# The order of splits, values and transposes at four layer boundaries of a two-block network on one core

## The chip, the cores and the metric

The kernel runs on one core of a Trainium2 chip. A core has five engines that run beside each other and meet only at semaphores: PE (TensorE, matrix products and transposes, writing to the accumulator memory `ps` of 8 banks), ACT (ScalarE), DVE (VectorE), POOL (GpSimd) and SP (SyncE, which here only issues the loads of the weights). Each engine takes its instructions in the order in which they are written for it. An instruction that waits for a semaphore keeps everything behind it on its engine waiting.

The metric is the device time of one execution in microseconds (us). Before the change three runs gave 1217.36, 1217.41 and 1218.13 us, median 1217.41 us.

## The reference

For 256 tokens of width 1024 the network computes two blocks in float32, one after the other, in seven stages: a gated feed-forward layer (FFN1), a mixing layer, a second gated layer (FFN2), then an attention layer (MoBA), a squared-ReLU layer (MLP1), a differential attention layer and a second squared-ReLU layer (MLP2). The four feed-forward layers are the ones that matter here:

```python
def _swiglu(x, w_in, w_out):            # FFN1, FFN2; hidden width 2816
    g, u = jnp.split(x @ w_in, 2, axis=-1)
    return (jax.nn.silu(g) * u) @ w_out

def sq_relu_mlp(h, w_up, w_down):       # MLP1, MLP2; hidden width 4096
    return jnp.square(jax.nn.relu(h @ w_up)) @ w_down

h = _swiglu(_rms_norm(x, ffn1_pre_norm[l]), ffn1_w_in[l], ffn1_w_out[l])
x = x + 0.5 * _rms_norm(h, ffn1_post_norm[l])
...
y = sq_relu_mlp(h, mlp_w_up[i], mlp_w_down[i])
x = layer_norm(DEEPNORM_ALPHA * x + (1.0 + gate2) * y, ln_g[i, 1], ln_b[i, 1])
```

## The kernel before

**Splitting.** Every float32 operand of a product is split into a high part, which the PE format holds, and the low rest. A product is three products: high by high, low by high, high by low (`three`, L506 to L508). Weights come in units of 128 x 2048 values (1 MB), N_UNITS in all, in a ring of six slots. Per unit SP issues the load (`w_raw`), ACT makes the high part (`split_hi`, L1047, `hi_w`), DVE the low part (`split_lo`, L1520, `lo_w`), and PE multiplies. SP may load a unit when PE has finished the one six before it. PE waits for a unit's low part (`low_ready`). A unit is 24 products: the 256 tokens are two tiles of 128, and each tile takes 12.

**The gated layer** (`swiglu`, one function of that name on each engine) goes over 11 blocks of 256 hidden columns. For a block PE multiplies two units (gate and up); ACT takes the silu of the gate (`activation`, L1152); DVE multiplies it with the up part (`product`, L1788, the tile `hid`); PE transposes the result (`hidden_T`, L634) into `ps`; ACT takes the high part of the transposed block (`hidden_hi`, L1160) and DVE the low part (`hidden_lo`, L1744); then PE multiplies it with the block's unit of the second weight. The last three blocks' second products are kept for the end (`down_tail`): first block N_FF - 3 on tile 0, then the transposes of block N_FF - 1, then blocks N_FF - 2 and N_FF - 1 on tile 0, then all three on tile 1. In what follows "the last block" is N_FF - 1 and "the last unit" is the weight unit that belongs to it (`next_unit - 1`).

At the end of the layer the written orders of ACT and DVE are:

```python
# ACT                                     # DVE
split_hi(next_unit - 1)                   split_lo(next_unit - 1)
hidden_hi(b0 + N_FF - 2, ...)             hidden_lo(b0 + N_FF - 2, ...)
activation(b0 + N_FF - 1, ...)            product(b0 + N_FF - 1, ...)
hidden_hi(b0 + N_FF - 1, ...)             if sums is not None: sums()
split_hi(next_unit)                       hidden_lo(b0 + N_FF - 1, ...)
split_hi(next_unit + 1)                   split_lo(next_unit), split_lo(next_unit + 1)
```

`sums` is `first_modulation`, in FFN2 alone: 15 small DVE instructions (L1777 to L1918) that finish the modulation vectors of the second block of the network. After these rows follows `after_rms`: DVE scales the layer's output out of `ps` (`rms_part`, L1603), computes the norm of tile 0, adds it to `x` (L1615), splits one more unit and then the new stage's input (`quarter_split`, L1553 to L1559). PE transposes `x` (`x_quarter_T`, L585) as two groups of four between the last products of `down_tail`, and waits for the L1615 half that each group reads.

**The squared-ReLU layer** (`mlp`) begins with `entry`: units 0, 1 and 2 of the layer for tile 0, then for tile 1. Units 0 and 1 give block 0 (banks 4 and 5), units 2 and 3 block 1 (banks 6 and 7). After `entry` PE transposes block 0 (`hidden_T(b0, 0, 4)`, eight transposes, L634), which waits for DVE's square (`product`, L1839); then it multiplies unit 3 for both tiles (`in_unit(u0 + 3, ...)`) and then units 4 and 5 with block 0's transposed values, for which it waits for `hidden_lo`. In MLP1 DVE also has pieces of a modulation product to do between its splits (L1757, L1760, L1767), right behind `hidden_lo`.

The code that matters:

Of the kernel before, what the change touches and what calls it, by code (L numbers as in the profile page):

```python
# [23 lines left out]
N_FF = D_FF // FF_B  # L24
# [119 lines left out]
def turned_up(j):  # L144
    return 4 * N_NAT - 2 + 2 * j - (j == N_TURN - 1)
# [6 lines left out]
def ring_slot(u):  # L152
    return u % RING
# [20 lines left out]
def two_blocks_kernel(nc, d, out):  # L174
    with ExitStack() as ctx:
# [108 lines left out]
        ffn_hT = [(hT_hi, hT_lo, 0), (hT_hi, hT_lo, 2), (hT2_hi, hT2_lo, 0)]  # L284
# [215 lines left out]
        def _(pe):  # L500
# [114 lines left out]
            def entry(u0, b, src):  # L615

                def second_tile_T():
                    x_quarter_T(b, 1, 0, src)
                    x_quarter_T(b, 1, 1, src)

                first_three = [(u0, 0, 0), (u0 + 1, 0, 1), (u0 + 2, 1, 0)]
                for u, block, half in first_three:
                    entry_unit(u, b, 0, block, half, second_tile_T if src is zt and block == 1 else None)
                    if src is x and half == 1:
                        second_tile_T()
                for u, block, half in first_three:
                    entry_unit(u, b, 1, block, half)
# [14 lines left out]
            def hidden_T(b, i, chunks):  # L642

                pe.wait_ge(hid_done, b + 1)
                transposes(hid, 0, chunks, (4 + 2 * (i % 2)) * BANK).then_inc(hidT, 1)
# [19 lines left out]
            xT = (xT_hi, xT_lo)  # L665
# [32 lines left out]
            def mlp(s, u0, b0, t0):  # L698
                def up_turned(j):

                    u, pair = u0 + turned_up(j), 4 + 2 * (j % 2)
                    if j < 2:
                        pe.wait_ge(hidT_lo, b0 + j + 1)
                    else:
                        pe.wait_ge(up_sum, t0 + j - 1)
                    low_ready(u)
                    whi = hi_w[:, ring_slot(u), :].rearrange("p (k f) -> p k f", k=KD)
                    wlo = lo_w[:, ring_slot(u), :].rearrange("p (k f) -> p k f", k=KD)
                    for f in range(2):
                        dst, cols = bank(pair + f), slice(f * P, (f + 1) * P)  # L710
                        for k in range(KD):
                            both = xT_both[:, k, :, :].rearrange("p s n -> p (s n)")
                            if k > 0:
                                pe.matmul(dst[:, 0:SEQ], wlo[:, k, cols], xT_hi[:, k, :], start=False, stop=False)  # L714
                            mm = pe.matmul(dst, whi[:, k, cols], both, start=k == 0, stop=k == KD - 1)  # L715
                            if k == 0:
                                pe.matmul(dst[:, 0:SEQ], wlo[:, k, cols], xT_hi[:, k, :], start=False, stop=False)
                    mm.then_inc(w_used, 1)

                def down_turned(j):  # L720
                    pe.wait_ge(turned_lo_done, t0 + j + 1)
                    down_unit(u0 + turned_down(j), turned_hT[j % 4], 0, False)

                entry(u0, s, zt)
                hidden_T(b0, 0, 4)
                in_unit(u0 + 3, xT, 4, [6, 7], False, True)
                for half in range(2):
                    pe.wait_ge(hidT_lo, b0 + 1)
                    down_unit(u0 + 4 + half, mlp_hT[0], 2 * half, half == 0)
                hidden_T(b0 + 1, 1, 4)  # L730
                for j in range(2):
                    up_turned(j)
                    pe.wait_ge(hidT_lo, b0 + 2)
                    down_unit(u0 + 7 + 2 * j, mlp_hT[1], 2 * j, False)
                for j in range(2, N_TURN - 2):
                    up_turned(j)
                    down_turned(j - 2)
                up_turned(N_TURN - 2)
                up_turned(N_TURN - 1)
                down_turned(N_TURN - 4)  # L740
                down_tail(s, [(u0 + turned_down(j), turned_hT[j % 4], 0, t0 + j) for j in range(N_TURN - 3, N_TURN)],
                          lambda: None, None if s == S_MLP2 else zt, turned_lo_done)
# [298 lines left out]
        def _(act):  # L1041
# [103 lines left out]
            def swiglu(u0, b0, n, between=None):  # L1145
# [33 lines left out]
                    if i == 3 and between is not None:  # L1179
                        between()  # L1180
                next_unit = u0 + 3 * N_FF
                split_hi(next_unit - 1)
                hidden_hi(b0 + N_FF - 2, N_FF - 2)
                activation(b0 + N_FF - 1, N_FF - 1)
                hidden_hi(b0 + N_FF - 1, N_FF - 1)
                split_hi(next_unit)
                split_hi(next_unit + 1)
# [319 lines left out]
        def _(vec):  # L1507
# [272 lines left out]
            def swiglu(u0, b0, first, p0, n_pieces, between=None, sums=None):  # L1780
# [34 lines left out]
                    if i == 3 and between is not None:  # L1815
                        between()
                next_unit = u0 + 3 * N_FF
                split_lo(next_unit - 1)
                hidden_lo(b0 + N_FF - 2, N_FF - 2, 2, ffn_hT[(N_FF - 2) % 3])
                product(b0 + N_FF - 1, N_FF - 1)  # L1820
                if sums is not None:
                    sums()
                hidden_lo(b0 + N_FF - 1, N_FF - 1, 2, ffn_hT[(N_FF - 1) % 3])
                split_lo(next_unit)
                split_lo(next_unit + 1)

# [675 lines left out]
```

## Time and profile before

| | |
|---|---|
| device time, median of 3 runs | 1217.41 us |
| the profiled execution: from its first to its last instruction (the only time that its page gives) | 1216.0 us |
| PE busy | 1199.6 us (99%), 5805 products and transposes |
| DVE busy | 950.8 us (78%) |
| ACT busy | 620.2 us (51%) |
| mean granted clock of PE | 0.997 of full |
| the chain that ended last | PE 88%, DVE 4%, ACT 3%, DMA 2% |
| data moved | 274.31 MB, mean 226 GB/s |

In the rows below a time is in us from the first instruction. A row of a timeline gives the start, the duration, the engine, the line, the operation, what it writes and reads, its shape, how many instructions it joins, and in brackets how long the engine had been idle before it and what ended that. Ends of PE instructions are modelled: products that follow each other show 0.39 us each and start 0.23 us apart. So a row's idle time on PE is counted from a modelled end. On ACT and DVE an instruction usually starts about 0.1 us before the end shown for the one ahead of it.

### The profile page before, as it was taken

How to read it: one execution, taken by the hardware profiler on the slowest of the kernel's cores; microseconds unless marked ns; L12 is line 12 of the kernel's file. 1: busy time of each engine (PE TensorE's matmuls, PEld its weight loads, DVE VectorE, ACT ScalarE, POOL GpSimd, SP SyncE). 2: the span in 40 equal slices, each digit the busy share in tenths (PEclk: the TensorE clock that was granted, in tenths of full speed). 3: DMA queues.
4: the chain of work that ended last, by engine and by line, in shares of the span. 5: the costliest groups of instructions: out<-in, count | busy, mean ns of one | idle time of the engine just before them, and what ended most of it. 6: DMA issues, size and time to landing. Idle time of an engine off the chain costs nothing.

```text
span 1216.0 us, 14811 instructions
## 1 busy us (share of the span) xinstructions
PE 1199.6 (99%) x5805; PEld 984.3 (81%) x5805; DVE 950.8 (78%) x1373; ACT 620.2 (51%) x844; POOL 83.0 (7%) x130
## 2 busy tenths in 40 slices
PE   9999999999999999999999999999999999999997
PEld 7888888888778888888887777888888777888885
DVE  7789878876766689889786668898998888765656
ACT  7345336445774464334465656443446565643441
POOL 2110130000300010000000000000100000000000
PEclk9999999999999999999999999999999999999998
DMA  9999995644645489989466347788856634566540
GB/s 317 352 319 321 311 300 185 221 143 155 200 157 175 156 295 349 317 307 333 150 219 225 106 127 254 269 305 281 312 193 215 217 114 139 174 217 216 185 162 35
DMA packets 145205, 274.31 MB, mean 226 GB/s; under 512 B 6240, under 2 KB 76080, under 8 KB 145136
## 3 DMA queue, kind: packets, MB, share of 16 engines
q1 hardware_dynamic: 127280, 209.80, 51.3%
q0 software_dynamic: 17792, 63.56, 15.2%
q8 instruction: 46, 0.75, 0.2%
q14 instruction: 23, 0.19, 0.0%
q10 hardware_dynamic: 64, 0.02, 0.0%
HBM read 270.41 MB, written 2.93 MB: 225 GB/s over the span
## 4 chain that ended last, share of the span: by engine, by line
PE 88%; DVE 4%; ACT 3%; DMA 2%; issue 2%; POOL 0%; ACTq 0%; DVEq 0%; POOLq 0%
PE ps L506 23%; PE ps L508 23%; PE ps L507 23%; PE ps L715 7%; PE ps L714 3%; PE ps L634 2%; DMA w_raw<-in_ffn_w_out 1%; ACT hi_w L1047 1%; DVE lo_w L1520 1%; PE ps L585 1%; PE ps L931 1%; DMA area<-rel_scratch 1%; ACT aux L1078 1%; PE ps L910 1%; PE ps L792 1%
## 5 line engine op out<-in xcount | busy, mean ns | idle before, releaser
L1520 DVE TENSOR_TENSOR lo_w<-w_raw,hi_w 128x2048 fp32r<-128x2048 f32 x195 | 443.5, 2287 | 65.7 <-ACT hi_w L1047 65.1
L1047 ACT ACTIVATE hi_w<-w_raw 128x2048 fp32r<-128x2048 f32 x195 | 370.3, 1916 | 46.6 <-DMA w_raw<-in_ffn_w_in 12.3
L506 PE MATMUL ps<-hi_w,xT 128*128 128x512 f32 x912 | 364.3, 399 | 2.2 <-DVE xT L1554 2.2
L508 PE MATMUL ps<-lo_w,xT 128*128 128x512 f32 x912 | 356.0, 390 | 0.0
L507 PE MATMUL ps<-hi_w,xT 128*128 128x512 f32 x912 | 355.3, 390 | 0.0
L506 PEld LDWEIGHTS ps<-hi_w,xT 128*128 128x128 f32 x912 | 171.3, 188 | 41.5 <-issue 8.1
L508 PEld LDWEIGHTS ps<-lo_w,xT 128*128 128x128 f32 x912 | 171.1, 188 | 37.0
L507 PEld LDWEIGHTS ps<-hi_w,xT 128*128 128x128 f32 x912 | 171.5, 188 | 33.4
L506 PE MATMUL ps<-hi_w,hT_hi 128*128 128x512 f32 x480 | 188.3, 392 | 0.0
L508 PE MATMUL ps<-lo_w,hT_hi 128*128 128x512 f32 x480 | 186.9, 389 | 0.0
L507 PE MATMUL ps<-hi_w,hT_lo 128*128 128x512 f32 x480 | 186.8, 389 | 0.0
L715 PE MATMUL ps<-xT,hi_w 128*128 128x512 f32 x384 | 134.6, 396 | 0.0
L508 PEld LDWEIGHTS ps<-lo_w,hT_hi 128*128 128x128 f32 x480 | 90.1, 188 | 19.1
L507 PEld LDWEIGHTS ps<-hi_w,hT_lo 128*128 128x128 f32 x480 | 90.1, 188 | 18.5
L506 PEld LDWEIGHTS ps<-hi_w,hT_hi 128*128 128x128 f32 x480 | 90.1, 188 | 18.0 <-issue 0.7
L714 PE MATMUL ps<-xT,lo_w 128*128 128x256 f32 x336 | 93.7, 279 | 0.0
L1760 DVE SCALAR_TENSOR_TENSOR piece_acc<-aux,c_act,piece_acc 128x512 f32<-128x512 f32 x119 | 89.3, 751 | 3.7
L1212 ACT ACTIVATE area<-ps 128x512 f32<-128x512 f32 x24 | 14.3, 597 | 135.3 <-PE ps L715 135.3
L715 PEld LDWEIGHTS ps<-xT,hi_w 128*128 128x128 f32 x384 | 70.2, 188 | 13.8
L1160 ACT ACTIVATE hT_hi<-ps 128x512 fp32r<-128x512 f32 x22 | 13.1, 598 | 107.2 <-PE ps L634 107.2
L714 PEld LDWEIGHTS ps<-xT,lo_w 128*128 128x128 f32 x336 | 63.3, 189 | 2.1
L1845 DVE TENSOR_TENSOR area<-ps,area 128x512 f32<-128x512 f32 x24 | 16.5, 689 | 48.8 <-ACT area L1212 48.8
(275 smaller groups left out, 1041.6 us busy)
## 6 DMA issues: line engine op xcount, KB each, us to landing
w_raw<-in_ffn_w_in SPq DMA_DIRECT2D x86, 512.0 KB
aux<-in_ada_w POOLq DMA_DIRECT2D x34, 1024.0 KB, 7.9
w_raw<-in_mlp_w_up SPq DMA_DIRECT2D x32, 1024.0 KB
w_raw<-in_mlp_w_down SPq DMA_DIRECT2D x32, 1024.0 KB
w_raw<-in_w_mix_in SPq DMA_DIRECT2D x26, 1024.0 KB
w_raw<-in_ffn_w_out SPq DMA_DIRECT2D x22, 1024.0 KB
area<-in_ada_w POOLq DMA_DIRECT2D x14, 1024.0 KB, 5.8
w_raw<-in_moba_w_in SPq DMA_DIRECT2D x12, 1024.0 KB
```

The costliest lines, as they stand in the source:

```text
L506: pe.matmul(dst, lhs_hi, rhs_hi, start=start, stop=False)
L507: pe.matmul(dst, lhs_lo, rhs_hi, start=False, stop=False)
L508: return pe.matmul(dst, lhs_hi, rhs_lo, start=False, stop=stop)
L634: mm = pe.transpose(ps[:, off:off + P], src[:, t, col0 + c * P:col0 + (c + 1) * P], ident[:, :])
L714: pe.matmul(dst[:, 0:SEQ], wlo[:, k, cols], xT_hi[:, k, :], start=False, stop=False)
L715: mm = pe.matmul(dst, whi[:, k, cols], both, start=k == 0, stop=k == KD - 1)
L1047: act.activation(hi_w[:, ring_slot(u), :], w_raw[:, ring_slot(u), :], ACT.Copy).then_inc(w_hi, 1)
L1160: act.activation(hi[:, c0:c0 + 2, :], ps[:, off:off + 2 * SEQ].rearrange("p (c n) -> p c n", c=2), ACT.Copy).then_inc(hidT_hi, 1)
L1212: act.activation(turned_lo, pair[:, :, 1, :], ACT.Copy).then_inc(up_low, 1)
L1520: vec.tensor_tensor(lo_w[:, ring_slot(u), :], w_raw[:, ring_slot(u), :], hi_w[:, ring_slot(u), :].bitcast(F32), ALU.subtract).then_inc(w_l ...
L1760: ins = vec.scalar_tensor_tensor(out=acc, in0=row, scalar=c_act[:, c:c + 1], in1=acc, op0=ALU.mult, op1=ALU.add)
L1845: vec.tensor_tensor(turned_sum, pair[:, :, 0, :], turned_lo, ALU.add).then_inc(up_sum, 1)
```

## The change

Three places are edited. In `mlp` on PE the two tiles of unit 3 (the layer's fourth) are taken apart and the transposes of block 0 stand between them. In the gated layer's end on ACT and on DVE, `split_hi` and `split_lo` of the last unit are written behind `activation` and `product` of the last block, and on DVE the last block's `hidden_lo` is written ahead of `sums`.

```diff
@@ PE, mlp
                 entry(u0, s, zt)
+                in_unit(u0 + 3, xT, 4, [6, 7], False, True, tiles=[0])
                 hidden_T(b0, 0, 4)
-                in_unit(u0 + 3, xT, 4, [6, 7], False, True)
+                in_unit(u0 + 3, xT, 4, [6, 7], False, True, tiles=[1])
@@ ACT, swiglu
                 next_unit = u0 + 3 * N_FF
-                split_hi(next_unit - 1)
                 hidden_hi(b0 + N_FF - 2, N_FF - 2)
                 activation(b0 + N_FF - 1, N_FF - 1)
+                split_hi(next_unit - 1)
                 hidden_hi(b0 + N_FF - 1, N_FF - 1)
@@ DVE, swiglu
                 next_unit = u0 + 3 * N_FF
-                split_lo(next_unit - 1)
                 hidden_lo(b0 + N_FF - 2, N_FF - 2, 2, ffn_hT[(N_FF - 2) % 3])
                 product(b0 + N_FF - 1, N_FF - 1)
+                split_lo(next_unit - 1)
+                hidden_lo(b0 + N_FF - 1, N_FF - 1, 2, ffn_hT[(N_FF - 1) % 3])
                 if sums is not None:
                     sums()
-                hidden_lo(b0 + N_FF - 1, N_FF - 1, 2, ffn_hT[(N_FF - 1) % 3])
                 split_lo(next_unit)
```

No instruction is added or taken away on any engine, and SP's order of loads is as it was. Line numbers behind the first edit are one higher in the changed kernel.

ACT at the end of FFN2 (FFN1's end reads the same): `hT_hi` is the high part of a transposed block, `area<-ps,rstd_x` the silu, `hi_w` a unit's high part. Before:

```order
L1047 ACTIVATE hi_w<-w_raw 128x2048 x2
L1160 ACTIVATE hT_hi<-ps 128x512
L1152 ACTIVATE area<-ps,rstd_x 128x256 x2
L1160 ACTIVATE hT_hi<-ps 128x512
L1047 ACTIVATE hi_w<-w_raw 128x2048 x2
```

And now:

```order
L1048 ACTIVATE hi_w<-w_raw 128x2048
L1161 ACTIVATE hT_hi<-ps 128x512
L1153 ACTIVATE area<-ps,rstd_x 128x256 x2
L1048 ACTIVATE hi_w<-w_raw 128x2048
L1161 ACTIVATE hT_hi<-ps 128x512
L1048 ACTIVATE hi_w<-w_raw 128x2048 x2
```

One of the two splits ahead has moved behind the last silu.

DVE at the end of FFN2: `lo_w` is a unit's low part, `hT_lo` that of a transposed block, `area<-ps,rstd_x,area` the product of silu and up part, `mod_cols` and `aff_*` the modulation. Before:

```order
L1520 TENSOR_TENSOR lo_w<-w_raw,hi_w 128x2048 x2
L1744 TENSOR_TENSOR hT_lo<-ps,hT_hi 128x512
L1788 SCALAR_TENSOR_TENSOR area<-ps,rstd_x,area 128x256 x2
L1777 TENSOR_TENSOR mod_cols<-ps,adab_cols 32x64 x4
...
L1918 TENSOR_TENSOR aff_b<-aff_b,mod_cols 128x8
L1744 TENSOR_TENSOR hT_lo<-ps,hT_hi 128x512
L1520 TENSOR_TENSOR lo_w<-w_raw,hi_w 128x2048 x2
L1603 SCALAR_TENSOR_TENSOR area<-ps,area 128x512 x2
```

And now:

```order
L1521 TENSOR_TENSOR lo_w<-w_raw,hi_w 128x2048
L1745 TENSOR_TENSOR hT_lo<-ps,hT_hi 128x512
L1789 SCALAR_TENSOR_TENSOR area<-ps,rstd_x,area 128x256 x2
L1521 TENSOR_TENSOR lo_w<-w_raw,hi_w 128x2048
L1745 TENSOR_TENSOR hT_lo<-ps,hT_hi 128x512
L1778 TENSOR_TENSOR mod_cols<-ps,adab_cols 32x64 x4
...
L1919 TENSOR_TENSOR aff_b<-aff_b,mod_cols 128x8
L1521 TENSOR_TENSOR lo_w<-w_raw,hi_w 128x2048 x2
L1604 SCALAR_TENSOR_TENSOR area<-ps,area 128x512 x2
```

One split now stands behind the product, and the modulation instructions stand between the last block's low part and the splits for the next stage.

On PE, in each of the two squared-ReLU layers, the eight transposes of block 0 now stand 12 products later than before, and nothing else differs.

## Rows read from the trace of the kernel before

**Rows 1.** What PE waited for, whole span: engine line, releaser, us in total, times, longest

```profile
PE ps L506 <- DVE xT L1554: 2.2, 2, 1.1
...
PE ps L634 <- DVE area L1788: 0.4, 1, 0.4
PE ps L634 <- DVE area L1839: 0.4, 2, 0.3
```

**Rows 2.** Timeline of PE at the end of FFN1

```profile
172.92 0.39 PE L508 MATMUL ps<-lo_w,xT 128*128 128x512 f32 x1
...
173.15 0.60 PE L634 MATMUL ps<-ident,area 128*128 128x128 f32 x4
...
182.39 0.66 PE L634 MATMUL ps<-ident,area 128*128 128x128 f32 x4 [0.43 <-DVE area L1788]
```

**Rows 3.** Timeline of ACT at the end of FFN1

```profile
176.71 1.92 ACT L1047 ACTIVATE hi_w<-w_raw 128x2048 fp32r<-128x2048 f32 x1 [6.16 <-DMA w_raw<-in_ffn_w_out]
...
179.28 0.84 ACT L1152 ACTIVATE area<-ps,rstd_x 128x256 f32<-128x256 f32 x2 [0.18 <-PE ps L508]
183.08 0.60 ACT L1160 ACTIVATE hT_hi<-ps 128x512 fp32r<-128x512 f32 x1 [2.96 <-PE ps L634]
```

**Rows 4.** Timeline of DVE at the end of FFN1

```profile
178.66 2.29 DVE L1520 TENSOR_TENSOR lo_w<-w_raw,hi_w 128x2048 fp32r<-128x2048 f32 x1 [5.78 <-ACT hi_w L1047]
...
181.47 0.87 DVE L1788 SCALAR_TENSOR_TENSOR area<-ps,rstd_x,area 128x256 f32<-128x256 f32 x2
...
185.52 4.49 DVE L1520 TENSOR_TENSOR lo_w<-w_raw,hi_w 128x2048 fp32r<-128x2048 f32 x2 [1.11 <-ACT hi_w L1047]
```

**Rows 5.** Timeline of ACT at the end of FFN2

```profile
586.20 3.71 ACT L1047 ACTIVATE hi_w<-w_raw 128x2048 fp32r<-128x2048 f32 x2
...
596.83 0.84 ACT L1152 ACTIVATE area<-ps,rstd_x 128x256 f32<-128x256 f32 x2 [4.88 <-PE ps L508]
```

**Rows 6.** Timeline of DVE at the end of FFN2

```profile
597.70 0.88 DVE L1788 SCALAR_TENSOR_TENSOR area<-ps,rstd_x,area 128x256 f32<-128x256 f32 x2 [4.45 <-ACT area L1152]
598.49 0.91 DVE L1777 TENSOR_TENSOR mod_cols<-ps,adab_cols 32x64 f32<-32x64 f32 x4
...
601.17 0.69 DVE L1744 TENSOR_TENSOR hT_lo<-ps,hT_hi 128x512 fp32r<-128x512 f32 x1
602.90 4.49 DVE L1520 TENSOR_TENSOR lo_w<-w_raw,hi_w 128x2048 fp32r<-128x2048 f32 x2 [1.04 <-ACT hi_w L1047]
607.31 1.28 DVE L1603 SCALAR_TENSOR_TENSOR area<-ps,area 128x512 f32<-128x512 f32 x2
...
610.41 1.42 DVE L1615 SCALAR_TENSOR_TENSOR x<-area,rstd,x 128x512 f32<-128x512 f32 x2
```

**Rows 7.** Timeline of PE where it first transposes the output of FFN2

```profile
610.97 0.39 PE L508 MATMUL ps<-lo_w,hT_hi 128*128 128x512 f32 x1
611.22 0.66 PE L585 MATMUL ps<-ident,x 128*128 128x128 f32 x4
```

**Rows 8.** Timeline of PE at the start of MLP1 (first three) and MLP2

```profile
749.18 1.09 PE L634 MATMUL ps<-ident,area 128*128 128x128 f32 x8 [0.26 <-DVE area L1839]
...
755.60 0.39 PE L506 MATMUL ps<-hi_w,hT_hi 128*128 128x512 f32 x1
...
772.96 0.39 PE L506 MATMUL ps<-hi_w,hT_hi 128*128 128x512 f32 x1
...
1045.84 1.09 PE L634 MATMUL ps<-ident,area 128*128 128x128 f32 x8 [0.15 <-DVE area L1839]
```

**Rows 9.** Timeline of DVE at the start of MLP1

```profile
751.37 1.23 DVE L1744 TENSOR_TENSOR hT_lo<-ps,hT_hi 128x1024 fp32r<-128x1024 f32 x1
...
769.02 1.22 DVE L1744 TENSOR_TENSOR hT_lo<-ps,hT_hi 128x1024 fp32r<-128x1024 f32 x1
```

**Rows 10.** Windows at the end: stretch, length, busy of PE, PEld, DVE, ACT, POOL, PEclk, DMA, GB/s

```profile
1207.50:1209.50 2.00, 0.00 (x0) 0.00 (x0) 1.93 (x3) 0.00 (x0) 0.00 (x0) 1.00 0.35 131
1210.00:1210.50 0.50, 0.00 (x0) 0.00 (x0) 0.50 (x2) 0.22 (x1) 0.00 (x0) 0.50 0.00 0
```

## The prediction

> **What bounds the kernel now.** I read the list of PE's waits first. PE is busy nearly all the time, so an edit of order can only win what PE still waits for, and three of those waits stand where the change works: one of 0.4 us behind L1788 and two of together 0.4 us behind L1839 [rows 1]. The other large entry, 2.2 us in two waits for `xT` (L1554), belongs to the starts of MLP1 and MLP2, ahead of the edited lines, and stays. That gives a ceiling for the gain before anything else is known.
>
> An idle time on PE is counted from a modelled end. Where nothing is waited for, transposes start 0.23 us after the last product's start (172.92 to 173.15 [rows 2]), though the product is drawn 0.39 us long. So a wait costs 0.39 - 0.23 = 0.16 us more than the row says: 0.43 + 0.16 = 0.59 us at the end of FFN1 [rows 2], 0.26 + 0.16 = 0.42 us at the start of MLP1 and 0.15 + 0.16 = 0.31 us at the start of MLP2 [rows 8]. FFN2's end has no such wait. The ceiling is 0.59 + 0.42 + 0.31 = 1.32 us.
>
> Then I read ACT, DVE and PE side by side at each of the four places, since on ACT and DVE an instruction holds up all that is written behind it.
>
> **End of FFN1, term 1.** The last unit's load lands late: ACT waits 6.16 us for it and starts the split at 176.71 [rows 3]. DVE follows at 178.66 with 2.29 us and only then makes the last block's product, at 181.47 for 0.87 us, which PE awaits at 182.39 [rows 2, 4]. Now the silu comes first. It is bound by PE, at 179.28 [rows 3], so it stays there; the product follows 0.87 us later, as in FFN2 (596.83 to 597.70 [rows 5, 6]): 180.15 + 0.87 = 181.0. PE is due at 182.39 - 0.59 = 181.80. The wait goes whole.
>
> What is late next: the last unit. Silu till 180.0, split 1.92 till 181.9, low part till 184.2, the last block's low part (0.69 [rows 6]) till 184.9. PE needs both after four transposes (0.4) and 12 products (12 x 0.23): 181.8 + 0.4 + 2.8 = 185.0. It fits by 0.1 to 0.2 us. The chain that follows (ACT's next high part at 183.08 [rows 3], DVE's next splits at 185.52 [rows 4]) starts from PE's transposes, so it moves up by the same 0.59 if the mixing layer's first two units have landed by then. They had at 183.6 and 185.4; whether they had 0.6 us sooner no row shows. Bounds: -0.59 and 0; I take -0.59, because the two splits ran back to back at 185.52 without a wait for a load.
>
> **End of FFN2, term 2.** Here the load is early. ACT does both splits from 586.20, ten microseconds ahead of the silu at 596.83 [rows 5], in time in which neither ACT nor DVE has anything else: DVE stands idle 4.45 us before its product [rows 6]. The change takes one split out of this free time and puts it behind the product, where DVE has little. Step by step, each instruction starting about 0.1 us before the drawn end of the one ahead:
> - ACT: silu till 597.6, split till 599.5.
> - DVE: product at 597.70 as before. Then it waits for the high part: low part of the unit from 599.50 (a split's low part starts some 1.95 after its high part) for 2.2 us to 601.7; low part of the last block, 0.61 on, to 602.3 (before it started at 601.17). PE needs these after its next 12 products, at about 603.0: in time.
> - The modulation instructions took from 598.49 to 601.17, 2.68 us [rows 6]. Before, they lay in the time in which PE and ACT made the last block's transposes and high part. Now: 602.32 + 2.68 = 605.00.
> - The next two splits start at 605.00 where they started at 602.90, after an idle 1.04 us which is used up [rows 6]. That is +2.10.
> - From there to L1615 DVE has no gap (602.90, 607.31, 610.41 [rows 6]): L1603 at 609.41, the first half of `x` from 612.51 to 613.2.
>
> Who waits for that: PE. The first L585 group starts at 611.22, 0.25 after the product before it [rows 7], so it is due at 611.20; its input was ready at 610.41 + 0.7 = 611.11, less than 0.1 us ahead. There is no cover at all. Now PE starts at about 613.26: +2.06 us. The rest of that stage hangs on the same DVE chain, moved by 2.10, and on PE, moved by 2.06, so it adds 0.04 at most. Nothing later gives it back: no later wait of PE in [rows 1] is for something that runs by its own clock; loads are released by PE's own progress. Bounds: 0, if DVE found the modulation's time elsewhere, and 2.10. I take +2.06.
>
> One row shows how strictly such a queue holds: in FFN1 ACT idled 6.16 us till 176.71 for a load, with the transposes of 173.15 already done for the instruction behind it [rows 2, 3]. The Trainium skill (Perfetto Trace Analysis, section Tensor Engine Instruction) says that ScalarE and VectorE are strict first-in first-out and that only the tensor engine may pull weight loads ahead. It is a rule against this change, and by it the sum keeps its +2.06; if ready instructions could pass a waiting one, that term would be near nothing.
>
> **Start of MLP1 and MLP2, terms 3 and 4.** The transposes come 12 products later, 12 x 0.227 = 2.72 us. PE then never waits for the square: it starts tile 0 of unit 3 at 749.18 - 0.42 = 748.76 and is at the transposes at 751.48, when the square has been ready since 749.13. The whole 0.42 goes, and 0.31 in MLP2. Unit 3 itself was split before the square.
>
> What is late next is `hidden_lo`, which PE needs at 755.60 - 0.42 = 755.18 [rows 8]. It started 751.37 - 749.18 = 2.19 us after the transposes [rows 8, 9]: 751.48 + 2.19 = 753.67, plus 1.23 is 754.9. It fits by 0.25 us, and likewise in MLP2. But in MLP1 DVE's queue behind it is full up to block 1's `hidden_lo`, 769.02 - 751.37 = 17.65 us later [rows 9]: now 753.67 + 17.65 + 1.23 = 772.55 plus 0.05 for the semaphore, and PE needs it at 772.96 - 0.42 = 772.54 [rows 8]. That gives back 0.06. Term 3 is -0.36 (bounds -0.42 and +0.1 if a load for the modulation comes later too), term 4 -0.31 (bounds -0.31 and 0).
>
> **The sum.** -0.59 + 2.06 - 0.36 - 0.31 = +0.80 us. On the profiled execution's span of 1216.0 us that is 1216.8. The median of the runs is 1217.41, 1.4 us more than the span, for what lies outside of the first and the last instruction; this part is untouched. So 1217.41 + 0.80 = 1218.2 us, slower by 0.07%. A measurement of this kernel can tell about 0.2%, or 2.4 us, from no change; this is not to be told.
>
> **The rivals.**
> - *The change does what its parts promise and no more.* If DVE's end of FFN2 has slack that I misread (the x chain's 0.1 us, the split's idle time), only the waits go: -1.3, 1216.1 us. For it: PE shows no wait at that place before. Against it: DVE's rows leave no gap from 602.90 to the transposes. Chance 0.12.
> - *The loss stays and the gains do not.* In FFN1 the mixing units' loads land no sooner, or the 0.1 us fits of FFN1, MLP1 and MLP2 fail and PE waits for low parts in place of products. Then +2.06 with gains of 0 to 0.5: 1217.41 + 1.8 = 1219.2 us. For it: every fit is tight, and FFN1's last load came 6 us late [rows 3]. Against it: the splits at 185.52 ran without a wait. Chance 0.12.
> - *The clock falls, and the change costs over 0.2%.* The place is the new gap at the end of FFN2. PE would stand 1.9 us (613.26 less the modelled end, 611.36), then do only four transposes. In the trace the clock was still full over 2.0 us of an empty PE after the last product, and at 0.50, which is 1.2 of 2.4 GHz, when PE had been empty for 2.5 to 3 us [rows 10]. My gap is just inside the first stretch; the case decides if the real one comes out longer than that. No row has a product at the low level; twice the spacing over 12 products would be 12 x 0.23 = 2.8 us more: 1218.2 + 2.8 = 1221.0. Chance 0.05. The Trainium skill (TensorE: Matmul & The Clock Gate, section HAM oscillation — how this bites in real kernels) says that a gap in PE's work can drop it to the half clock and that the kernel then pays each time for warming up; by the same page (Part 4: PE-mode transpose) transposes do not count as such work. By that rule the transposes would lengthen the gap.
>
> **How the numbers follow.** The forecast, with FFN2's loss and most gains, has 0.68; its own range is 1217.5 to 1218.8. The rivals have 0.12, 0.12 and 0.05, and 0.03 is left for what I do not see. The range 1216.2 to 1219.8 holds the forecast, the second rival and about half of the first. Faster by over 2.4 us would need more than all waits at the edited places: 0.01. Slower by over 2.4 us is the clock's case and part of the second and of the rest: 0.08. Within: 0.91.
>
> **What would show it.** In the profile after: PE's waits behind L1789 and L1840 are gone; a new wait of about 1.9 us stands before L585, for DVE's L1616, at about 612 us; DVE's L1604 in FFN2 follows the modulation instructions with two splits and no idle time; DVE's block-1 `hT_lo` in MLP1 starts about 2 us later than now. The prediction is wrong in its main step if L585 shows no wait there, and in its small ones if PE waits for `hT_lo` or `lo_w` at the other three places. A granted clock under 1.00 near 613 us would speak for the last rival.

## The result, and the profile after

The changed kernel takes 1219.65 us (median of 21 executions, 1218.34 to 1221.22), the kernel before in the same series 1217.59 us (21 executions, 1216.79 to 1219.07). The ratio is 1.0017 with a 95% interval of 1.0011 to 1.0022: slower by 2.06 us. The forecast was 0.80 slower, 1218.2. The direction was right, but the loss is two and a half times as large. The measured time lies inside the stated range by 0.15 us only, and outside of the forecast's own 1217.5 to 1218.8. The forecast also held the change too small to be told from none; with 21 executions of each kernel the interval lies above 1.

The profiled execution of the changed kernel spans 1217.8 us, that of before 1216.0. The first two rows of after's list of PE's waits (engine line, releaser, us in total, times, longest):

```profile
PE ps L506 <- DVE xT L1555: 2.2, 2, 1.1
PE ps L585 <- DVE x L1616: 2.0, 1, 2.0
```

Both rows before L634 that the change aims at, three waits [rows 1], are off the list, and a new wait of 2.0 us stands before L585. The rest is found by reading the same places as before.

**End of FFN1.** ACT, DVE and PE of after:

```profile
178.93 0.84 ACT L1153 ACTIVATE area<-ps,rstd_x 128x256 f32<-128x256 f32 x2 [4.89 <-PE ps L508]
179.65 1.92 ACT L1048 ACTIVATE hi_w<-w_raw 128x2048 fp32r<-128x2048 f32 x1
```
```profile
179.80 0.88 DVE L1789 SCALAR_TENSOR_TENSOR area<-ps,rstd_x,area 128x256 f32<-128x256 f32 x2 [5.04 <-ACT area L1153]
...
184.52 4.49 DVE L1521 TENSOR_TENSOR lo_w<-w_raw,hi_w 128x2048 fp32r<-128x2048 f32 x2
```
```profile
181.45 0.60 PE L634 MATMUL ps<-ident,area 128*128 128x128 f32 x4
```

The product follows the silu by 0.87 us and no longer the load's split; PE starts its transposes without idle time. The next two splits start 1.00 us sooner than in [rows 4]; 0.35 of that is this execution's earlier start (its transposes before these came at 172.80, in before at 173.15), the other 0.65 is the wait of 0.59 that is gone and 0.06 that has no name here.

**End of FFN2.** DVE of after, to be laid beside [rows 6]:

```profile
596.73 0.88 DVE L1789 SCALAR_TENSOR_TENSOR area<-ps,rstd_x,area 128x256 f32<-128x256 f32 x2 [5.03 <-ACT area L1153]
598.54 2.29 DVE L1521 TENSOR_TENSOR lo_w<-w_raw,hi_w 128x2048 fp32r<-128x2048 f32 x1 [0.93 <-ACT hi_w L1048]
600.75 0.68 DVE L1745 TENSOR_TENSOR hT_lo<-ps,hT_hi 128x512 fp32r<-128x512 f32 x1
601.35 0.91 DVE L1778 TENSOR_TENSOR mod_cols<-ps,adab_cols 32x64 f32<-32x64 f32 x4
...
603.92 4.48 DVE L1521 TENSOR_TENSOR lo_w<-w_raw,hi_w 128x2048 fp32r<-128x2048 f32 x2
608.43 1.29 DVE L1604 SCALAR_TENSOR_TENSOR area<-ps,area 128x512 f32<-128x512 f32 x2
...
611.54 1.42 DVE L1616 SCALAR_TENSOR_TENSOR x<-area,rstd,x 128x512 f32<-128x512 f32 x2
```

Everything here starts 0.97 us earlier on the clock of the span, by its earlier start and the wait won in FFN1 (597.70 to 596.73). Counted from the product, the next two splits come 7.19 us later (603.92 less 596.73) and came 5.20 later before (602.90 less 597.70): +1.99. On the way to L1616 0.11 more is added (7.62 us against 7.51). From 598.54 on DVE has no idle time over 0.04 us. The forecast had +2.10 for the first part and nothing for the second: the modulation took 2.57 us here (601.35 to 603.92) in place of the 2.68 that it counted.

PE of after at the new wait, to be laid beside [rows 7]:

```profile
610.00 0.39 PE L508 MATMUL ps<-lo_w,hT_hi 128*128 128x512 f32 x1
612.35 0.65 PE L585 MATMUL ps<-ident,x 128*128 128x128 f32 x4 [1.96 <-DVE x L1616]
612.76 0.63 PE L506 MATMUL ps<-hi_w,hT_hi 128*128 128x512 f32 x1
613.19 0.63 PE L507 MATMUL ps<-hi_w,hT_lo 128*128 128x512 f32 x1
...
615.32 1.06 PE L585 MATMUL ps<-ident,x 128*128 128x128 f32 x4
616.03 0.61 PE L506 MATMUL ps<-hi_w,hT_hi 128*128 128x512 f32 x1
616.48 0.39 PE L507 MATMUL ps<-hi_w,hT_lo 128*128 128x512 f32 x1
...
623.10 1.03 PE L585 MATMUL ps<-ident,x 128*128 128x128 f32 x8
```

The last row is the next group of eight transposes. In the kernel before it is this one:

```profile
620.38 1.18 PE L585 MATMUL ps<-ident,x 128*128 128x128 f32 x8
```

Two things are to be seen. The wait is where the forecast put it. And behind it the products stand 0.43 us apart in place of 0.23, until 616.48; the second four transposes are drawn 1.06 us long, where before's at 613.10 are drawn 0.60. The windows of PE there (stretch, length, PE busy, granted clock, DMA share, GB/s) say why:

```profile
606.00:612.00 6.00, 4.39 (x20) 1.00 0.13 14
612.00:612.50 0.50, 0.15 (x1) 1.00 0.56 127
612.50:613.00 0.50, 0.50 (x5) 0.92 0.89 319
613.00:616.00 3.00, 3.00 (x11) 0.50 0.65 251
616.00:616.50 0.50, 0.50 (x4) 0.66 0.00 0
616.50:622.00 5.50, 5.50 (x26) 1.00 0.99 338
```

The granted clock was 1.00 through the idle time, fell to 0.50 (1.2 of 2.4 GHz) just as the products had begun again, and was back at 1.00 from 616.5. A window's mean tells the moment: 0.92 over half a microsecond is a fall at 612.9, which is 2.9 us after the start of the last product ahead of the gap, and 0.66 is a return at 616.3. That is the mechanism of the third rival, on top of the forecast and not in its place.

**Start of MLP1.** PE and DVE of after beside [rows 8, 9]:

```profile
754.04 1.03 PE L634 MATMUL ps<-ident,area 128*128 128x128 f32 x8
...
757.65 0.39 PE L506 MATMUL ps<-hi_w,hT_hi 128*128 128x512 f32 x1
...
775.03 0.50 PE L506 MATMUL ps<-hi_w,hT_hi 128*128 128x512 f32 x1
```
```profile
756.17 1.23 DVE L1745 TENSOR_TENSOR hT_lo<-ps,hT_hi 128x1024 fp32r<-128x1024 f32 x1 [2.22 <-ACT hT_hi L1204]
...
773.76 1.22 DVE L1745 TENSOR_TENSOR hT_lo<-ps,hT_hi 128x1024 fp32r<-128x1024 f32 x1
```

No idle time before the transposes; `hT_lo` is done at 757.40, a quarter of a microsecond ahead of L506 at 757.65; for block 1 it is done at 774.98, and PE, which started its product before that at 774.75 and was due at 774.98, starts at 775.03: the 0.05 late that the forecast counted as 0.06.

**The ledger.** Lengths on PE between the same instructions in both profiled executions, in us:

| from, to | before | after | difference | forecast |
|---|---|---|---|---|
| FFN1, transposes of the last block but one to those of the last | 9.24 | 8.65 | -0.59 | -0.59 |
| FFN2, transposes of the last block to the first L585 | 11.39 | 13.49 | +2.10 | +2.06 |
| that L585 to the next group of eight | 9.16 | 10.75 | +1.59 | 0 |
| MLP1, first L585 to the transposes of block 1 (`hidden_T(b0 + 1, 1, 4)`) | 37.76 | 37.25 | -0.51 | -0.42 |
| MLP2, the same | 37.99 | 37.62 | -0.37 | -0.31 |
| all the rest, first product to last | | | -0.06 | 0 |

MLP1's stretch ends ahead of the product that is 0.05 late; taken up to that product (772.96 in before, 775.03 here) the difference is -0.49, and the forecast's -0.36.

From the first product of FFN1 (10.90 in before) to the last it is 1196.18 before and 1198.34 after: +2.16. (The spans differ by 1.8, since the first product of this execution came 0.39 us sooner.)

### The profile page after: what moved, and what is told of

Its sections match the earlier page's. It is cut to its first block, busy times and chain, and to the rows that moved or that the text cites. A ratio compares the mean times of both kernels' runs of the same rounds, so it can differ in the third digit from the quotient of the medians.

```text
span 1217.8 us, 14811 instructions
## 1 busy us (share of the span) xinstructions
PE 1200.8 (99%) x5805; PEld 986.0 (81%) x5805; DVE 950.5 (78%) x1373; ACT 620.4 (51%) x844; POOL 83.1 (7%) x130
## 4 chain that ended last, share of the span: by engine, by line
PE 90%; DVE 5%; ACT 2%; issue 2%; DMA 0%; ACTq 0%; DVEq 0%
PE ps L506 24%; PE ps L508 24%; PE ps L507 24%; PE ps L715 7%; PE ps L714 3%; PE ps L634 2%; ACT hi_w L1048 1%; DVE lo_w L1521 1%; PE ps L585 1%; PE ps L932 1%; PE ps L911 1%; PE ps L793 1%; PE ps L909 1%; ACT area L1331 1%; DVE area L2017 0%
## 5 line engine op out<-in xcount | busy, mean ns | idle before, releaser
L506 PE MATMUL ps<-hi_w,xT 128*128 128x512 f32 x912 | 364.1, 399 | 2.2 <-DVE xT L1555 2.2
L506 PEld LDWEIGHTS ps<-hi_w,xT 128*128 128x128 f32 x912 | 171.3, 188 | 41.6 <-issue 7.9
L506 PE MATMUL ps<-hi_w,hT_hi 128*128 128x512 f32 x480 | 189.0, 394 | 0.0
L506 PEld LDWEIGHTS ps<-hi_w,hT_hi 128*128 128x128 f32 x480 | 90.4, 188 | 18.7 <-issue 0.9
```

Source lines behind the costliest of these rows:

```text
L506: pe.matmul(dst, lhs_hi, rhs_hi, start=start, stop=False)
```

## The experiments

All times are medians with the lowest and highest execution and, in brackets, the number of executions. The three series (e1 to e4, e5 to e8, e9 to e11) ran on three chips, so each ratio is to the kernel before on the same chip. The kernel before, run beside them three times, gave 1217.53 (e1 to e4), 1217.51 (e5 to e8) and 1217.45 us (e9 to e11).

### e1: the changed kernel again

> The changed kernel once more, on the chip of the next three. Theory (queue and clock): DVE's modulation work now stands ahead of the next stage's splits at the end of FFN2, PE stands 2.0 us before L585, the granted clock falls to 0.50 about 2.5 us after the last product, and seven products and four transposes run at half speed: span about 1.8 us over before, and the runs scatter, because the low clock lasts longer or shorter. Rival (queue alone): 0.8 us over before, with no scatter.

1219.79 us, 1218.43 to 1221.30 (11), ratio 1.0019 (1.0010 to 1.0027). Its trace has the wait of 1.95 us before L585 and the next group of eight 10.74 us later (10.75 in after). The loss repeats.

### e2: two unread products in the gap

```diff
 # PE, down_tail
                 if src is x and i < 2:
+                    if i == 0 and s == S_FFN2:
+                        for _ in range(2):
+                            pe.matmul(ps[:, 5 * BANK:5 * BANK + SEQ], piece_acc[:, 0, 0:P],
+                                      piece_acc[:, 0, SEQ:2 * SEQ], start=True, stop=True)
                     x_quarter_T(s + 1, 0, i, src)
```

> The changed kernel with two float32 products of 128 x 256 whose result nobody reads, on PE ahead of the first transposes of x at the end of FFN2, inside the wait. They need about 1.5 us of the 2.1. Queue and clock: the wait for DVE's x stays (L585 starts as late as in the changed kernel), the clock stays at 1.00, and the time is 1.6 us under the changed kernel, 0.5 to 0.8 us over before. Queue alone, where the low clock is only a companion of something else that slows PE: no gain, or a loss of the products' time.

1218.54 us, 1218.22 to 1220.35 (11), ratio 1.0010 (1.0001 to 1.0018): 1.25 below e1. PE of this kernel (each unread product is recorded as two instructions):

```profile
610.67 1.02 PE L573 MATMUL ps<-piece_acc 128*128 128x256 f32 x4
612.79 0.66 PE L589 MATMUL ps<-ident,x 128*128 128x128 f32 x4 [1.09 <-DVE x L1620]
613.20 0.48 PE L506 MATMUL ps<-hi_w,hT_hi 128*128 128x512 f32 x1
613.51 0.39 PE L507 MATMUL ps<-hi_w,hT_lo 128*128 128x512 f32 x1
```

The queue's part stays (13.49 us from the last block's transposes to this group, as in after), and the clock's part goes: products at 0.23 us and 9.16 us to the next group, as before. So the loss has two parts, and the second can be taken away alone. Four of the eleven executions still lie at 1219.5 to 1220.4.

### e3 and e4: FFN2 left as before

e3 is the changed kernel with the written order of before in FFN2 alone (`if u0 == U_FFN1` around the moved lines); e4 has the edit of the squared-ReLU layers alone.

> The change with the end of FFN2 left as before: the new order at the end of FFN1 and the new place of the transposes in MLP1 and MLP2. Queue and clock: -0.59 (FFN1), -0.42 (MLP1; -0.36 if the block-1 low part comes late as in the changed kernel) and -0.31 (MLP2): 1.3 us under before, no wait of PE before L585. Rival (the gains are absorbed by loads that come no sooner): the same time as before within 0.3 us.

> Only PE's edit in MLP1 and MLP2. Both theories: -0.42 or -0.36 and -0.31, together 0.7 us under before; in MLP1 DVE's block-1 low part is ready 0.05 us after PE wants it. If the transposes' later place costs more than it frees (the low part late for units 4 and 5): a wait of PE for hT_lo at the first product of unit 4.

e3: 1216.37 us, 1216.11 to 1217.45 (11), ratio 0.9990 (0.9981 to 0.9999). e4: 1216.42, 1216.05 to 1217.83 (11), ratio 0.9991 (0.9982 to 1.0000). The loss sits in FFN2 and the rest of the change gains. In e3's trace FFN1's stretch is 8.65 us, FFN2's 11.39, MLP1's 37.30 and MLP2's 37.59. But e4 was to be 0.6 slower than e3 and is not. In its trace FFN1's stretch is 8.91 us, though e4 has the old order there: the wait that the forecast read as 0.59 was 0.26 here. Nor was e4 to gain more than 0.7, and it gained 1.1; its trace has 0.89 of that at MLP1 and MLP2 (37.28 and 37.58 us). The rest no trace shows.

### e5: only the low part ahead of the modulation

```diff
 # DVE, swiglu, from before
                 product(b0 + N_FF - 1, N_FF - 1)
+                hidden_lo(b0 + N_FF - 1, ...)
                 if sums is not None:
                     sums()
-                hidden_lo(b0 + N_FF - 1, ...)
```

> The kernel before with one edit in FFN2 alone: DVE's low part of the last block stands ahead of the modulation instructions, the last unit's split stays early. If an instruction that waits holds up all behind it: DVE idles from 598.5 till the high part is there (600.97 in before), low part till 601.6, the modulation's 2.66 us till 604.3, the next splits start at 604.3 to 604.4 in place of 602.90, and PE's L585 is 1.4 to 1.5 us late. The clock then decides the rest. If a gap has to be about as long as in the changed kernel (L585 2.1 us late) to lower it, products behind L585 keep 0.23 us spacing and the median is before +1.5, about 1219.0. If any gap of this kind with only transposes behind it lowers the clock, some 1.6 us more: 1220.6. Rival to the queue (DVE finds the modulation's time elsewhere): no change, 1217.5.

1218.80 us, 1218.14 to 1220.18 (11), ratio 1.0010 (1.0001 to 1.0019): 1.3 over before. DVE of this kernel:

```profile
597.67 0.88 DVE L1788 SCALAR_TENSOR_TENSOR area<-ps,rstd_x,area 128x256 f32<-128x256 f32 x2 [4.46 <-ACT area L1152]
601.08 0.69 DVE L1744 TENSOR_TENSOR hT_lo<-ps,hT_hi 128x512 fp32r<-128x512 f32 x1 [2.52 <-ACT hT_hi L1160]
601.68 0.91 DVE L1777 TENSOR_TENSOR mod_cols<-ps,adab_cols 32x64 f32<-32x64 f32 x4
...
604.25 4.49 DVE L1520 TENSOR_TENSOR lo_w<-w_raw,hi_w 128x2048 fp32r<-128x2048 f32 x2
```

DVE now idles 2.52 us for the high part with the modulation ready behind it: the clearest row on how a queue holds. L585 comes 12.87 us after the last block's transposes (612.68 less 599.81), +1.48; 1.4 to 1.5 was expected. Its products behind L585 are at full pace and the windows there show 1.00: a stretch of 2.14 us from one product to the next (610.95 to 613.09) did not lower the clock in this execution, and nine of the eleven lie at 1218.1 to 1219.2, where +1.5 puts them.

### e6: the modulation behind the next splits too

```diff
 # DVE, swiglu, from after
-                if sums is not None:
-                    sums()
                 split_lo(next_unit)
                 split_lo(next_unit + 1)
+                if sums is not None:
+                    sums()
```

> The changed kernel with one more edit in FFN2: the modulation instructions stand behind both splits for the next stage. DVE: next splits again at 602.9, the modulation between them and L1604, so all 2.66 us of it are added ahead of L1604 and L585 is 2.7 us late (changed kernel 2.1). By the queue alone that is +0.6 over the changed kernel, about 1220.2. If the clock's cost is one fixed piece once it falls, it stays there, with low products behind L585 in most executions (1220.2). If the cost grows with the length of the gap, or comes in more of the executions, 1220.8 to 1222, and the low stretch in the trace starts no later than in the changed kernel but lasts longer. If the clock did not matter, the changed kernel's medians would also be reached here with 0.6 more and all products 0.23 us apart.

1220.71 us, 1219.14 to 1222.24 (9), ratio 1.0027 (1.0018 to 1.0037); 1220.2 was expected if nothing but the queue's 0.6 is added. L585 comes 14.08 us after the last block's transposes, +2.69 over before, as expected. PE of this kernel:

```profile
610.51 0.39 PE L508 MATMUL ps<-lo_w,hT_hi 128*128 128x512 f32 x1
613.45 0.66 PE L585 MATMUL ps<-ident,x 128*128 128x128 f32 x4 [2.54 <-DVE x L1616]
613.86 0.48 PE L506 MATMUL ps<-hi_w,hT_hi 128*128 128x512 f32 x1
...
614.64 0.60 PE L506 MATMUL ps<-hi_w,hT_hi 128*128 128x512 f32 x1
615.04 0.63 PE L507 MATMUL ps<-hi_w,hT_lo 128*128 128x512 f32 x1
```

The gap is 0.59 us longer than in after, and the fall costs the same: 10.77 us to the next group of eight (624.22 less 613.45), 1.61 over the 9.16 of before. The expectation that the low stretch would start no later was wrong: the first three products still ran at full pace, and it began at 614.66, 4.1 us after the last product before the gap, against 2.9 in after. The same trace holds a second fall, at the start of MLP2, where nothing was changed.

### e7: the squared-ReLU edit undone

> The changed kernel with the edit of the squared-ReLU layers undone (transposes of block 0 again ahead of unit 3). Theory: the two waits behind L1839's square come back and cost 0.42 + 0.31 = 0.73 us by the rows of before (0.89 by the segments of the two traces); everything at FFN1 and FFN2 stays as in the changed kernel: 1219.7 + 0.8 = 1220.5, and the MLP segments in the trace as long as before. Rival: these waits are hidden by something else, no change to the changed kernel, 1219.7.

1220.26 us, 1218.84 to 1221.31 (10), ratio 1.0021 (1.0012 to 1.0030): 0.6 over after, 0.8 expected. Its trace was not what I expected. The gap at FFN2 is as in after (610.50 to 613.25 between products, PE idle 1.95 us), and the clock did not fall there: 9.20 us to the next group of eight. But MLP2's stretch, from the first L585 to block 1's transposes, took 39.27 us in place of 37.99. PE there, and the windows (columns as in [rows 10]):

```profile
1025.65 0.39 PE L508 MATMUL ps<-lo_w,xT 128*128 128x512 f32 x1
1026.64 1.36 PE L585 MATMUL ps<-ident,area 128*128 128x128 f32 x8 [0.60 <-ACT area L1093]
1029.08 0.77 PE L506 MATMUL ps<-hi_w,xT 128*128 128x512 f32 x1 [1.07 <-DVE xT L1554]
1029.64 0.63 PE L507 MATMUL ps<-hi_w,xT 128*128 128x512 f32 x1
```
```profile
1028.00:1029.00 1.00, 0.00 (x1) 0.00 (x0) 0.79 (x3) 1.00 (x4) 0.00 (x0) 1.00 0.97 393
1029.00:1029.50 0.50, 0.42 (x1) 0.46 (x2) 0.47 (x2) 0.50 (x3) 0.00 (x0) 0.52 1.03 426
1029.50:1032.00 2.50, 2.50 (x7) 1.93 (x7) 2.42 (x5) 0.74 (x3) 0.00 (x0) 0.50 0.37 151
1032.00:1032.50 0.50, 0.50 (x2) 0.41 (x2) 0.50 (x2) 0.00 (x0) 0.00 (x0) 0.57 0.00 0
1032.50:1040.00 7.50, 7.50 (x38) 6.00 (x37) 3.35 (x12) 3.62 (x9) 0.00 (x0) 1.00 0.00 0
```

So the clock falls at the old wait of 1.1 us as well, and in some executions only: of the ten traces without added products at MLP2's start this one and e6's have a fall there. The kernel before has the same waits; its own trace has no fall at them. A gap is a chance of a fall, and the fall has a size.

### e8: FFN1's new order alone

> The kernel before with the new order of split and silu/product in FFN1 alone. Theory: the wait before the last block's transposes goes where the last unit's load is late; the segment from the transposes before (about 173) to these (about 182) is 8.65 us long instead of 9.24, and the median falls by 0.2 to 0.6, since the load is not equally late in every execution: 1217.0 to 1217.3. Rival: the chain behind it (the mixing layer's first loads) gives it back: segment shorter, but the one behind it longer by as much, median 1217.5.

1216.94 us, 1216.74 to 1217.56 (11), ratio 0.9993 (0.9984 to 1.0002). The stretch in FFN1 is 8.65 us and the one behind it (transposes to L585) 11.45, as long as elsewhere (11.44 in e5, 11.40 in e9). The gain is not given back. It cannot be told from no change by the interval; the median is 0.57 under before. This 0.57 and e4's 1.11 add up to more than the 1.16 of e3, which has both edits. So part of each is something that the median of before has and those of all three have less of (see "Left open").

### e9 to e11: unread products at the starts of MLP1 and MLP2

```diff
 # PE, entry_unit, ahead of the wait for xT
+                if t == 0 and block == 0 and half == 0 and b in (S_MLP1, S_MLP2):
+                    for _ in range(3):
+                        pe.matmul(ps[:, 5 * BANK:5 * BANK + P], ident[:, :], ident[:, :], start=True, stop=True)
```

e9 is the kernel before with this, e10 is e3 with this, e11 is the changed kernel with this and with the products of e2.

> The kernel before with three float32 products of ident with ident (128x128, result unread) ahead of PE's wait for xT at the start of MLP1 and of MLP2, inside the idle 1.1 us. About a third of all executions of before so far are 1.3 to 1.9 us longer than the rest (1218.3 to 1219.2 against 1216.8 to 1217.9) and show a mean clock of 0.996. Theory: in these the clock fell once at the start of MLP1 or MLP2, where 2.7 to 3 us pass between two products, as one trace (e7) shows. Then here no execution lies above 1218.0 or shows 0.996, and the median is 1217.3, some 0.2 under before, since those 1.1 us of waiting stay. Rival: the long executions come from elsewhere (loads, start), and a third of them stays above 1218.3.

> The new order in FFN1 alone and the edit of the squared-ReLU layers (as in e3, 1216.37), and the three products of e9 at the start of MLP1 and MLP2. Theory: 1216.3, and no execution above 1217.0, since only falls of the clock lengthened those (two of 11 in e3, 1217.04 and 1217.45). This should be the fastest of all here, about 1.2 under before. Rival: the added products delay the first product of each layer; each by up to 0.3 us would show as a longer stretch there, 1216.9.

> The changed kernel with idle products at all three places: two 128x256 ones ahead of the transposes in FFN2's gap (as in e2, 1218.54) and three 128x128 ones at the start of MLP1 and of MLP2. Theory: e2 still had four of 11 executions at 1219.5 to 1220.4, from falls at the squared-ReLU layers' starts; here all lie at 1218.1 to 1218.8 and the median is 1218.4, which is before without falls (1217.3) plus the queue's 2.1 less gains of 1.0. Rival: other causes of scatter, and a third of the executions stays above 1219.3.

| kernel | median | lowest to highest | ratio to before |
|---|---|---|---|
| before, beside them (27) | 1217.45 | 1216.82 to 1218.88 | |
| e9 (11) | 1217.17 | 1217.02 to 1217.87 | 0.9997 (0.9988 to 1.0006) |
| e10 (11) | 1216.30 | 1215.97 to 1216.74 | 0.9989 (0.9980 to 0.9997) |
| e11 (11) | 1218.34 | 1218.21 to 1218.77 | 1.0007 (0.9998 to 1.0015) |

PE of e9 at the start of MLP1 (again two instructions for each added product): the added products fill most of the wait, and the first product is not late (2.39 us after L585, 2.47 before):

```profile
728.25 1.36 PE L585 MATMUL ps<-ident,area 128*128 128x128 f32 x8
729.46 0.83 PE L596 MATMUL ps<-ident 128*128 128x128 f32 x6
730.64 0.50 PE L506 MATMUL ps<-hi_w,xT 128*128 128x512 f32 x1 [0.35 <-DVE xT L1557]
```

The long executions are gone from all three, as expected. Of the 90 executions of before in the three series 24 lay above 1218.1 us, of e9's eleven none; after and e1 spread over 3 us (1218.34 to 1221.30), e11 over 0.6. The intervals in the table are wider than these steps, but the executions of the three kernels, all on one chip, do not overlap (e10 ends at 1216.74, e9 begins at 1217.02 and ends at 1217.87, e11 begins at 1218.21). So their medians can be laid side by side: e11 less e9, the whole change, is +1.17; e11 less e10, FFN2's queue alone, is +2.04; e10 less e9, the gains, is -0.87. e10 is the fastest kernel here, 1.15 us under before and 3.4 under the changed one.

With this the executions of the changed kernel read as three groups. Of 32 (after and e1) six lie at 1218.3 to 1219.0, no fall; twenty at 1219.3 to 1220.4, one; six at 1220.9 to 1221.3, two. The mean granted clock, measured for each execution, parts them in the same way: 0.998 in all of the first group, 0.997 in all of the second, 0.995 in all of the third, where one low stretch of 3.4 us at 0.50 should take 0.0014 off. So 26 had a fall somewhere; the place is shown in the traces of after, e1, e6 and e7 alone. e6 has one, four and four.

Falls are not all of the scatter. The expectation of e10 took the two longest of e3, 1217.04 and 1217.45, for falls; the one at 1217.04 is the profiled execution, and its granted clock is 1.00 to the last product. What differs there is the start: FFN1's first product comes at 11.63 us in e3's trace and at 10.72 in e10's (1216.35 us). Over the thirteen traces it comes at 10.28 to 11.63, so the start alone can move a time by up to 1.3 us.

## Why the prediction was right and wrong

- **Term 2, FFN2's queue** (+2.06): right in mechanism, place and size. The trace has +2.10 (1.99 up to the next splits and 0.11 between them and L1616, where 2.10 and nothing were reckoned), the medians without falls +2.04. e5 and e6 move it to +1.48 and +2.69 as the same reckoning says. DVE's slack of 1.04 us was used up, and the x chain's 0.1 us was no cover.
- **Term 1, FFN1** (-0.59): the mechanism is right and this pair of traces even has the size, but the size was one draw. Four kernels with the old order there, all profiled once, had 9.24 (before), 8.91 (e4), 8.91 (e5) and 8.65 us (e9) for a stretch that is 8.65 without a wait: the wait was 0.59, 0.26, 0.26 and 0. What varies is the load: ACT began the last unit's split 3.56 us after the transposes before it in before [rows 2, 3], 3.23 in e4 and e5, 2.44 in e9, so a split 0.33 us sooner made the wait 0.33 shorter. With the new order all nine traces have 8.65. Against the mean of 0.28 the term was 0.3 too large. I had given it bounds of -0.59 and 0 and taken the end that the single trace showed.
- **Terms 3 and 4, MLP1 and MLP2** (-0.36, -0.31): right, and a little small. Up to block 1's transposes, where the reckoning has -0.42 and -0.31, the traces have -0.51 and -0.37; e3's have -0.46 and -0.40. Block 1's low part is 0.05 late behind them, as reckoned. Most of what is missing is in the transposes: eight that followed a wait were drawn 1.09 us long [rows 8] and are 1.03 without one.
- **The clock** (left out of the sum, chance 0.05, price 2.8): this is the step that failed, though the time lies inside the range. The mechanism was named and its place was right, but its chance and its price were wrong. I set the gap of 1.9 us against the 2.0 us in [rows 10], over which an idle PE still had the full clock, and took that for a threshold. It is none. One trace shows one draw: in that trace the clock fell 2.8 us after the last product of all had begun, and in the other twelve, at the same place with PE empty all the while, 2.5 (e9) to 4.9 us after it (e3). Between products the stretch was 2.76 us in after, with four transposes in it, and the clock fell; it did in e1's trace, with 2.75, and did not in e7's, also with 2.75. That it fell there in most executions is an estimate: 26 of 32 executions had a fall somewhere, and where the gap was filled (e2) four of eleven. Nor is the price two spacings for 12 products: it was 1.59, 1.58 and 1.61 us in after, e1 and e6, because the clock came back after 3.4 us. e2 took it away and won 1.25 in the median.
- **The median of before**: it holds falls already. The forecast added the sum to 1217.41 and took the scatter of the three runs for nothing. It also read 1.4 us between the span (1216.0) and the median as what lies outside of the span; in every execution with both numbers that part is 1.8 to 1.9 us. So the profiled execution of before took about 1217.8, 0.4 over the median that the sum started from, and its wait of 0.59 in FFN1 is the longest of four. Without falls before is about 1217.17 (e9, whose MLP1 stretch is 0.08 shorter for another reason, 37.68 us), and it lies 0.42 higher by the median of 1217.59; after lies 1.31 above its own 1218.34. So the measured +2.06 is +1.17 without the clock and 0.89 more for it. The forecast of +0.80 is to be held against +1.17, and the difference of 0.37 has FFN1's 0.3 as its nearest cause; medians of two series cannot show it to a tenth.
- **The rivals**: that the change only gains is refuted by the wait before L585. That the loss stays and the gains do not is refuted by e3, e4 and e10, which gain 0.87 to 1.16. The third was the one to weigh higher, not instead of the forecast but as a further term of it: 1217.41 + 0.80 + 1.6 = 1219.8, against 1219.65. That this comes so near is luck: the start is 0.24 too high, the sum 0.37 too low, and the falls add 1.31 to the changed kernel's median and not 1.6.
- **The range**: that 1219.65 is inside is luck too. Its upper end, 1219.8, was set to take in the second rival, whose mechanism (no gains) is refuted. The clock's case was to lie above it, at 1221.0, and came in under it because one fall costs 1.6 and not 2.8.

**Left open.** Why falls were rarer in e3, e4 and e8 (3 of 33 executions over 1 us above their median) than in before beside them (17 of 63 over 1 us above theirs), though the waits at MLP1 and MLP2 are the same, no run here tells, nor what decides whether a given gap brings a fall. A fall of before itself was not caught in a trace. That its long executions are falls rests on their mean granted clock (of the 24 above 1218.1 us 17 show 0.996, five 0.997 and two 0.998; of the other 66 only one is under 0.997); that they are at the starts of MLP1 or MLP2 rests on e9, and on e6's and e7's traces, both at MLP2. None was seen at MLP1.

## What to carry to other kernels

An early place in a queue that costs nothing there may be holding a later chain: before an instruction is moved behind something, add up all that stands between it and the next one that the bottleneck waits for, since a queue with 1 us of slack cannot take in 3. A new gap on TensorE has two prices, its own length and a possible fall of the clock behind it, and the second comes in some executions and not in others: look at the spread of the executions and at several traces before taking one trace's full clock, or one trace's wait for a load, for the rule. Where such a gap could not be closed, a few unread products in it cost nothing here and took the second price away (e2, e9, e11).

## What the runs showed of the hardware that I had not expected

- The fall has one size in all five that were caught: the clock at 0.50 for 3.4 us (612.9 to 616.3 in after, 1029.0 to 1032.4 in e7). It cost 1.6 us at FFN2. At MLP2's start in e7 the 30 products behind it also took 1.58 us longer than in before, but 0.30 of that came back by the end of the stretch, 0.23 of it at the second group of L585: it had waited in before (it started 0.46 us after the product ahead) and no longer did (0.23). What is left is 1.28.
- It can come when PE has started again: 2.9 us after the last product ahead of the gap in after, and 4.1 us in e6, where three products had already run at full pace. In e7 it came 3.4 us after it, 0.06 before the next product.
- Transposes slow down as products do: four took 1.06 us in place of 0.60, and started 0.21 us apart in place of 0.11 (615.32, 615.53, 615.75, 615.96 in after).
- The waits of 1.1 us at the starts of MLP1 and MLP2, with eight transposes ahead of each, make most of before's own scatter of 2.4 us. From one product to the next it is 2.7 us at MLP1 and 3.4 at MLP2. With three unread products in each (e9) the scatter is 0.85, and the median 0.3 lower.
